# The last block of each attention pair inside the next slot, and its reciprocals by transfer

## The reference, cut to what matters

```python
p = jnp.exp(s - m)
denom = jnp.sum(p, axis=-1, keepdims=True)
if sink is not None:
    denom = denom + jnp.exp(sk - m)
out = jnp.einsum('nbhgqk,nbkhd->nbqhgd', p / denom, vb.astype(jnp.float32))
...
ya = ya.reshape(b, seq, A_W) * jax.nn.silu(za)
```

## Time and profile before

| | |
|---|---|
| runs | 3627.81 us median of 3 (3623.05 to 3629.15) |
| profiled execution | 3626.68 us, its span 3624.9 us |
| PE busy | 3431.3 us (95%) |
| DVE, ACT, POOL busy | 51%, 22%, 33% |
| attention pairs | 1600 to 2140 us (first layer), 2700 to 3165 us (second, roughly) |
| granted TensorE clock, mean | 0.979 |

### The profile page before, as it was taken

How to read it: one execution, slowest core, us unless ns; L and a number is a source line. 1 busy time by engine, 2 the same in 40 slices (tenths; PEclk the granted TensorE clock), 3 DMA queues, 4 the chain that set the end, 5 groups by cost and what they waited for, 6 DMA issues and landing times.

```text
span 3624.9 us, 55702 instructions
## 1 busy us (share of the span) xinstructions
PE 3431.3 (95%) x22740; PEld 2766.9 (76%) x22740; DVE 1858.6 (51%) x2512; ACT 783.5 (22%) x1234; POOL 1186.5 (33%) x557
## 2 busy tenths in 40 slices
PE   5999699999999999989999999999999999999997
PEld 4888489788888888866777678888867677688886
DVE  6531566556666676664544444343545444534434
ACT  3311433211100101133322220000323332300001
POOL 2333054233344344322222224344322222243442
PEclk9999799999999999989999999999999999999998
DMA  3121000121111111131111111111311111111111
GB/s 111 53 69 46 0 4 4 51 87 47 46 46 52 46 46 48 44 112 47 36 35 41 35 70 48 51 46 47 112 53 41 41 35 30 69 47 53 46 46 64
DMA packets 50942, 181.94 MB, mean 50 GB/s; under 512 B 5600, under 2 KB 14304, under 8 KB 49520
## 3 DMA queue, kind: packets, MB, share of 16 engines
q1 hardware_dynamic: 36432, 135.85, 11.8%
q10 hardware_dynamic: 14368, 43.98, 3.6%
HBM read 157.73 MB, written 14.75 MB: 48 GB/s over the span
## 4 chain that ended last, share of the span: by engine, by line
PE 89%; DVE 7%; issue 1%; ACT 1%; DMA 1%; POOL 0%; ACTq 0%; DVEq 0%; SPq 0%; POOLq 0%
PE ps L465 54%; PE ps L901 10%; PE ps L1257 5%; PE ps L1077 3%; PE ps L1104 3%; PE ps L731 3%; PE ps L1122 3%; DVE sc L2486 1%; PE ps L929 1%; PE ps L1143 1%; PE ps L1031 1%; DVE sq_sum L1837 1%; PE ps L484 0%; PE ps L478 0%; DMA pv<-vec 0%
## 5 line engine op out<-in xcount | busy, mean ns | idle before, releaser
L363 POOL TENSOR_TENSOR wH<-wraw,pv 128x1024 fp32r<-128x1024 f32 x239 | 460.5, 1927 | 2183.0 <-PE ps L465 1781.4
L465 PE MATMUL ps<-hH,wH 128*128 128x512 f32 x2800 | 878.1, 395 | 20.8 <-issue 13.6
L465 PE MATMUL ps<-hL,wH 128*128 128x512 f32 x2800 | 870.9, 392 | 0.0
L465 PE MATMUL ps<-hH,wL 128*128 128x512 f32 x2800 | 870.2, 392 | 0.0
L365 POOL TENSOR_TENSOR wL<-wraw,wH 128x1024 fp32r<-128x1024 f32 x239 | 622.8, 2606 | 18.8
L465 PEld LDWEIGHTS ps<-hH,wH 128*128 128x128 f32 x2800 | 523.0, 189 | 136.3 <-issue 24.1
L465 PEld LDWEIGHTS ps<-hL,wH 128*128 128x128 f32 x2800 | 527.5, 189 | 110.5
L465 PEld LDWEIGHTS ps<-hH,wL 128*128 128x128 f32 x2800 | 525.9, 189 | 109.6
L2284 DVE TENSOR_TENSOR xT<-ps,xT 128x512 f32<-128x512 f32 x560 | 372.2, 689 | 11.1 <-PE ps L929 11.0
L2579 DVE TENSOR_TENSOR sg<-ps,mrows 128x1024 f32<-128x1024 f32 x46 | 56.3, 1225 | 371.6 <-PE ps L465 371.6
L1703 ACT ACTIVATE sc<-sc,stat 128x256 f32<-128x256 f32 (+7 forms) x256 | 171.0, 668 | 133.7 <-DVE stat L2493 66.1
(11 more groups left out here) (392 smaller groups left out, 4249.7 us busy)
## 6 DMA issues: line engine op xcount, KB each, us to landing
wraw<-ws SPq DMA_DIRECT2D x242, 512.0 KB, 3.5
park<-xT ACTq DMA_DIRECT2D x2, 4096.0 KB, 13.2
xT<-park ACTq DMA_DIRECT2D x2, 4096.0 KB, 12.9
xT<-xin SPq DMA_DIRECT2D x1, 4096.0 KB, 12.2
xT<-xin ACTq DMA_DIRECT2D x1, 4096.0 KB, 12.2
sc<-kraw ACTq DMA_DIRECT2D x32, 128.0 KB, 2.4
out<-xT SPq DMA_DIRECT2D x8, 512.0 KB, 3.5
sc<-qraw ACTq DMA_DIRECT2D x24, 128.0 KB, 2.4
```

Source lines behind the costliest of these rows:

```text
L363: pool.tensor_tensor(wH[:, j, :], wraw[:, j, :], zero, ALU.add).then_inc(w_hi, 1)
L465: mm = pe.matmul(pair(p)[:, half * HALF:(half + 1) * HALF], wp, hp[:, k, half * HALF:(half + 1) * HALF], start=(m == 0 and n == 0), stop=( ...
```

## The change

- **PE.** `period(7)` and what follows leave the end of the pair. `pair_end` makes three pieces of them: transposes(7, 0) with values(6); transposes(7, 1); values(7) with one transposition of `stat[S_REC]` (16 columns) into 16 rows of bank 4. `col_gemm` of the next query slot (for the last B pair the key slot of `window_keys`) calls them behind its pairs 3, 6 and 11, in C 2, 4 and 8 (from 0). The last C pair of a layer keeps period 7, `rows` and `values(7)` where they were. The transposes of block 7 for head 1 go to PSUM pair 1 instead of 0. The waits for `at_y` stand later: in front of the value transposes (A, B) or of the rotation (C).
- **DVE.** `output` multiplies the PSUM output by the gate alone. A new step `output_scale` multiplies `ypair` by `recT` (the reciprocal rows) once they have come; it and the low part stand behind the query step of the next pair (A), the query rotation (B), the key rotation of `window_keys`, or after blocks 1 and 3 of the next pair (C).
- **ACT.** `spread_reciprocals` copies the 16 rows (`rec_rows`), sends them to a stretch of `out` in DRAM, waits, and issues two transfers that bring each row set to 64 partitions of `recT`. `output_hi` (the high part) moves behind the swap of the queries, before the copy of the keys (B), before the copy of the values (`window_keys`), or after block 3's exponentials (C, at n = 2).
- `qraw2` moves to the place of `vst2`, since `ypair` is alive longer; in B, ACT's copy of the values therefore waits for the query rotation. The C pairs are written out instead of looped. Some semaphores share a name (`gate`, `pool_own`, `rw_tanh`) and nothing else there changes.

```diff
...
-        qraw2 = at("qraw2", XA + 4 * TILE, [P, T])
+        qraw2 = at("qraw2", XA, [P, T])
...
+        rec_rows = at("rec_rows", EX3 + 4 * TILE + 2432, [16, P])
+        recT = at("recT", YL, [P, KT, T])
...
-                col_gemm(0, u)
-                pe.wait_ge(sem("at_y"), pi + 1)
+                col_gemm(0, u, between=pair_end("B", L, 2, 2))
                 col_gemm(1, u)
                 pe.wait_ge(sem("a_raw"), L * 14 + 11)
+                pe.wait_ge(sem("at_y"), pi + 1)
                 pe.wait_ge(sem("a_v"), L * 6 + 6)
...
-                        out, b = pair(0 if n == 7 and j else 2), 0
+                        out, b = pair(1 if n == 7 and j else 2), 0
...
+            def pair_end(br, L, i, first):
+
+                _, transposes, values, _ = steps(br, L, i, first)
+
+                def last_block():
+                    transposes(7, 0)
+                    values(6)
+
+                def values_and_rows():
+                    values(7)
+                    pe.wait_ge(sem("at_rec"), L * 8 + i + (first + 1))
+                    pe.transpose(bank(4)[0:16, 0:P], stat[:, S_REC, :], ident).then_inc(sem("at_rows"), 1)
+
+                at = (2, 4, 8) if br == "C" else (3, 6, 11)
+                return {at[0]: last_block, at[1]: lambda: transposes(7, 1), at[2]: values_and_rows}
+
+            def head_pair(br, L, i, first, ended={}):
+                pi = L * 8 + i + first
+                last = pi * 16
+                scores, transposes, values, period = steps(br, L, i, first)
...
-                pe.wait_ge(sem("at_max"), last + 1)
+                pe.wait_ge(sem("at_max"), last + (2 if br == "C" else 1))
                 if br == "C":
                     u = L * (LAYER_SLOTS // 2) + i + ((SLOT_LAYER + SLOT_WINDOW) // 2 + 1)
-                    col_gemm(0, u)
+                    col_gemm(0, u, between=ended)
 
                     def rotate_q():
                         pe.wait_ge(sem("a_raw"), L * 14 + i + 12)
+                        pe.wait_ge(sem("at_y"), pi + 1)
+                        pe.wait_ge(sem("rec_copied"), spreads(L, i + first))
...
+                        if not leading:
+                            pe.wait_ge(sem("at_y"), pi + 1)
+                            pe.wait_ge(sem("rec_copied"), spreads(L, i + first))
...
-                        col_gemm(*slots[0], p=0)
-
-                        pe.wait_ge(sem("at_y"), pi + 1)
+                        col_gemm(*slots[0], p=0, between=ended)
                         col_gemm(*slots[1], p=1)
...
-                for n in range(within, 8):
+                ends_here = br == "C" and i == 2
+                for n in range(within, 8 if ends_here else 7):
                     period(n)
-                rows()
-                values(7)
+                if ends_here:
+                    rows()
+                    values(7)
...
-                    if br == "A":
+                    if br != "B":
                         for i in range(count):
-                            head_pair(br, L, i, first)
+                            head_pair(br, L, i, first, pair_end(br, L, i - 1, first) if i else {})
                         continue
                     with pe.Fori(0, count) as i:
-                        head_pair(br, L, i, first)
+                        head_pair(br, L, i, first, pair_end(br, L, i - 1, first))
...
+            def output_hi(L, i):
+
+                pi = L * 8 + i
+                act.wait_ge(sem("at_scaled"), pi + 1)
+                act.sem_inc(sem("gate"), 1)
+                act.activation(yH[:, bass.ds(i, 1), :], ypair[:, :].unsqueeze(1), ACT.Copy).then_inc(sem("a_yH"), 1)
+
+            def spread_reciprocals(L, i):
+
+                n = spreads(L, i)
+                act.wait_ge(sem("at_rows"), L * 8 + i + 1)
+                act.activation(rec_rows[:, :], bank(4)[0:16, 0:P], ACT.Copy).then_inc(sem("rec_copied"), 1)
+                act.wait_ge(sem("rec_copied"), n + 1)
+                act.dma_start(out[0:1, 4:6, :].rearrange("o k (r q) -> (o k r) q", q=P), rec_rows[:, :]
+                              ).then_inc(sem("rec_kept"), 16)
+                act.wait_ge(sem("rec_kept"), n * 16 + 16)
+                for j in range(2):
+                    act.dma_start(recT[64 * j:64 * j + 64, bass.ds(i, 1), :],
+                                  out[0:1, 4 + j:5 + j, :].to_broadcast([64, 1, T])).then_inc(sem("rec_spread"), 16)
...
-                act.wait_ge(sem("a_yL"), L * 8 + 6)
+                act.wait_ge(sem("at_y"), L * 8 + 6)
                 act.activation(lnM[:, :], arows[:, :], ACT.Copy)
                 act.wait_ge(gemm_done[0], u + 1)
                 raw_copy(kraw2, 0)
                 swap_halves(kraw2, 1, L * 14 + 11)
+                output_hi(L, 4)
                 act.wait_ge(gemm_done[1], u + 1)
...
                         swap_halves(qraw2, 0, raw + 1)
+                        output_hi(L, i + (first - 1))
...
+                        if n == 2 and i:
+                            output_hi(L, i + (first - 1))
...
-                act.wait_ge(sem("at_y"), pi + 2)
-                act.sem_inc(sem("act_gate"), 1)
-                act.activation(yH[:, bass.ds(i + first, 1), :], ypair[:, :].unsqueeze(1), ACT.Copy).then_inc(sem("a_yH"), 1)
+                if br == "C" and i == 2:
+                    output_hi(L, i + first)
+                else:
+                    spread_reciprocals(L, i + first)
...
+            def output_scale(L, i):
+
+                dve.wait_ge(sem("rec_spread"), spreads(L, i) * 32 + 32)
+                dve.wait_ge(sem("at_y"), L * 8 + i + 2)
+                dve.tensor_tensor(ypair[:, :].unsqueeze(1), ypair[:, :].unsqueeze(1), recT[:, bass.ds(i, 1), :], ALU.mult
+                                  ).then_inc(sem("at_scaled"), 1)
+
+            def output_low(L, i):
+
+                dve.wait_ge(sem("a_yH"), L * 8 + i + 1)
+                dve.tensor_tensor(yL[:, bass.ds(i, 1), :], ypair[:, :].unsqueeze(1), yH[:, bass.ds(i, 1), :],
+                                  ALU.subtract).then_inc(sem("a_yL"), 1)
+
             def window_keys(L):
                 rope(L, L * 10 + 6, L * 14 + 11, swaps(L, 7), SC[1][:, 1, :], SC[1][:, 1, :], kraw2, kP)
+                output_scale(L, 4)
+                output_low(L, 4)
...
+                        if q == 0:
+                            output_scale(L, i + (first - 1))
+                            output_low(L, i + (first - 1))
...
-                    dve.wait_ge(sem("at_rows"), pi + 1)
                     dve.wait_ge(sem("a_z"), pi * 2 + 2)
-                    st.on(dve.tensor_tensor(sz[:, :], pair(1), sz[:, :], ALU.mult))
-                    st.wait(dve)
+                    if ends_here:
+                        dve.wait_ge(sem("at_rows"), pi + 1)
+                        st.on(dve.tensor_tensor(sz[:, :], pair(1), sz[:, :], ALU.mult))
+                        st.wait(dve)
                     dve.wait_ge(sem("at_pv"), pi * 8 + 8)
-                    dve.scalar_tensor_tensor(out=ypair[:, :], in0=pair(3), scalar=0.5, in1=sz[:, :], op0=ALU.mult, op1=ALU.mult
-                                             ).then_inc(sem("at_y"), 1)
+                    ins = dve.scalar_tensor_tensor(out=ypair[:, :], in0=pair(3), scalar=0.5, in1=sz[:, :],
+                                                   op0=ALU.mult, op1=ALU.mult)
+                    ins.then_inc(sem("at_y"), 1)
...
+                    if n == 1 and br == "C" and i:
+                        output_scale(L, i + (first - 1))
+                    if n == 3 and br == "C" and i:
+                        output_low(L, i + (first - 1))
...
```

More of the change, by code:

```diff
@@ L302, in bias_copies, with spreads @@
             return 4 + (L * 2 + i) * 6
+        def spreads(L, i):
+            return L * (KT - 1) + i
         def head_slots(L, br, i):
@@ L386, in _ @@
             zero_slot(SLOT_OUT // 2 - 1)
-            own = Count(sem("pool_own"))
+            own = Count(sem("pool_own"), 1)
             def step(ins):
@@ L649, in gate @@
             def gate():
-                pe.sem_inc(sem("pe_gate"), 1)
+                pe.sem_inc(sem("gate"), 1)
             def rows(q):
@@ L1134, in period @@
                         scores(n + 1)
+                return scores, transposes, values, period
+            def pair_end(br, L, i, first):
[13 more added lines that the diff above has]
+                scores, transposes, values, period = steps(br, L, i, first)
                 def rows():
@@ L2433, in head_pair @@
                 buffers = 4 if br == "C" else 2
-                st = Count(sem("dve_own"), L * 11 + own.n + (i * 2 + 5 if br == "C" else i + first))
+                st = Count(sem("dve_own"), L * 4 + own.n + i)
                 if br == "A":
@@ L2508, in copy_transposed @@
                         dve.wait_ge(sem("at_pv"), pi * 8 + n - 1)
-                    src = bank(5) if n < 4 else pair(2 if n < 7 else 0)
+                    src = bank(5) if n < 4 else pair(2 if n < 7 else 1)
```

49 lines of the change are left out of this document (30 added, 19 removed).

## The result

The changed kernel takes **3578.5 us** (median of 4 runs, 3575.6 to 3578.8), the kernel before in the same session 3625.4 (4 runs): a ratio of 0.987, 95% interval 0.986 to 0.989. Forecast were 3592 us and a range from 3580 to 3606.

A forecast was written before the change was run, and what follows sets the result against it. The prediction took PE (TensorE), 89% of the chain, as the bound. Moved ends gain 38.7 us, less 1.1 and 1.5 is 36.1; from 3626.7 that gives 3590.6, plus 1.1 for the median: 3592 us, range 3580 to 3606.

The forecast's parts named there:

- rival 1: Moved blocks: PE's waits for exponentials and copies move with them into the next slot; 16 us gained, 3612; chance 0.10.
- rival 4: Moved ends: entering and leaving costs 0.11 us more at each of nine switches; about 3617 to 3622; chance 0.04.
- rival 3: Reciprocals' trip through memory is long and delays ACT, DVE, then PE; 3654 us at a 20 us trip; chance 0.04.
- prices of the blocks: PE's moved blocks, priced start to start from the old kernel; A or B end gains 2.72 us, C end 2.88.
- window_keys: ACT's high part of the last B pair delays its values copy, so PE waits: 0.55 us each layer, 1.1 lost.
- The low part in C: C pairs 1 and 2: DVE's low part delays block 5's maxima; 0.37 us, four times, 1.5 lost.
- rival 5: Whole kernel: window_keys and C losses absorbed (2.6 us), two to four slow stretches vanish (up to 6); 3583; chance 0.07.
- 0.1 more a switch: Moved ends on PE: possible extra cost per switch, up to 6 us, part of the forecast's own spread of some 8.
- PE feels it only if ... past 27.8: A or B slot: trip hidden up to 13.8 us unless scale, high part and low part delay ACT's k copy.
- just free: ACT in an A or B slot: held about 5 us by the trip, free when the slot's copy comes at 16.9.
- Of which 25 are the matmuls of L1143: Old pair ends on PE: 25 of 38.7 us gained come from removing 32 small matmuls that spread the reciprocals.
- Rival 2: Thinner, interrupted slots bring one slower-clock stretch per moved end, 1.65 us each; 23 of 36 us lost, 3615; chance 0.05.

The follow-up runs named there:

- second profile of the changed kernel: The changed kernel run again without any edit, with a profile: 3578.1 us, 0.987 of the kernel before.
- The runs with long waits of PE: The changed kernel with four more waited 8 KB writes, ahead of the reads of the reciprocals (3633.9 us) or behind their issue (3640.8 us).

## Where the prediction was right, and which of its steps failed

**Right: the mechanism on PE.** PE sets the time, its blocks find their inputs inside the next slot, the holes do not move with them (rival 1), the returns cost about what was read (rival 4), and the trip stays hidden (rival 3 did not happen).

**Failed: the sizes.** The time fell out of the range on the fast side because terms of the sum were mis-sized, above all the prices of the blocks and the two losses that did not come. The 14 us by which 3592 is too high come from these steps:

1. *Prices of the blocks (A and B ends: 2.72 counted, 3.0 and 3.2 measured).* I priced every block by its place in the kernel before. In front of a gemm the transposes are cheaper: 0.74 and 0.79, where the step "eight transposes 1.02, so seven 0.89" had 0.89 and 1.02. The row transposition takes 0.03 instead of 0.13, the last products 1.90 instead of 1.84. Together 6.11 against 6.58. The returns come to 0.53 in all instead of 0.44, about as read. Ten ends: 31, where the sum had 27.2.
2. *window_keys (1.1 counted, 0 measured).* The step added 1.23 of scale behind the end of the rotation. DVE's operations in a row start every 1.14 us, and that layer's wait for the swap was longer in the profile of before (3.41) than after (2.67). The high part was done 0.3 us before PE had the slot ready.
3. *The low part in C (1.5 counted, 0 measured).* The 0.37 was taken as if all of it reached PE. 0.09 did, and the next wait gave 0.08 back. C ends: 2.80 measured for the end itself (16.84 to 14.04 from the last transposes of block 6 to the query copy; 2.88 counted), 12.0 for four whole pairs where the sum had 10.0. The 2.80 hold a wait that the prediction had at nothing: in front of each of the four slots PE waits 0.24 for the maxima of block 7, for which the edit raised the wait to `last + 2`.
4. *The last C pair of each layer* had no term; it got 0.4 to 0.5 us shorter, twice (34.64 to 34.15 us from its query copy to the merge in the first layer).
5. *The base.* Median and profiled execution of the kernel before lay on the high side of its later runs: 3625.4 over 4 runs, 3623.9 over 19.

2.4 for the base, 3.8 for the blocks, 1.1 and 2.0 for the losses that did not come, and 0.8 make 10.1 of 13.5 us. Some 3 us are left, of which the clock can be 2; the others stay open.

**The range** had room for rival 5 (3583), which was that the losses of steps 2 and 3 are absorbed (they were) and that slow stretches vanish, which the profiles don't show (22.2 against 25.6 and 17.0). What it lacked was an error of the block prices in the gain's direction: "0.1 more a switch" was the only side I had put in.

**The budget was wrong though its outcome was right, and that was luck.** The step "PE feels it only if ... past 27.8", 13.8 us for the trip, took DVE's wait for the rows as what decides. The trip took some 6.5 us where 9 were counted, and no wait of DVE for it is in the trace. Its two transfers (DMA issues: count, KB each, median us to landing):
```profile
recT<-out ACTq DMA_DIRECT2D x28, 256.0 KB, 3.9
...
out<-rec_rows ACTq DMA_DIRECT2D x14, 8.0 KB, 1.4
```
But with about 12 us of trip the gain was already gone. What decides is ACT, held behind its own write: it was free at about 1817.8 and copied the q slot at 1820.3 (second profile of the changed kernel), a room of 2.5 us, and 0.3 to 0.7 us behind the high part at the extra projection. It was held 3.0 us where the prediction had 5 and "just free". The prediction saw that point and did not carry it on. Rival 3 priced 20 us of trip at 3654; 12 us gave 3634. The Trainium skill, DMA: Bandwidth & Descriptors, Anatomy of one DMA, puts about 2 us of fixed cost on a transfer, in its part on transfers that GpSimd issues; the prediction took the figure without that condition. ScalarE issues the 8 KB write here, and it took a median of 1.4 us, so the trace is below the figure.

**"Of which 25 are the matmuls of L1143"** was right for the ends already moved and only so (27.1 measured). Alone in place they bring 5 to 6.

**Rival 2** (the slower level spreads with the switches) falls: 22.2 us not granted in both profiles after, 17.0 and 25.6 before. The runs with long waits of PE had 39 and 49, so the stretches seem to go with waits more than with switches; no run varied the one without the other.

## What to carry to other kernels

Before you take work off the engine that sets the time, look at what waits behind it: matmuls that stand between a transposition and its use may cover the copy, and then their removal pays only once the block stands where other work covers it. A block's price depends on its neighbour in the queue, so price a move with rows that have the new neighbour. And budget a trip through memory by the queue of the engine that waits for its write, not only by who reads the result: here a delay of 1.4 us was nearly free and one of 5.5 us cost the whole gain.

## What the runs showed of the hardware

- The same eight transposes take 0.97 to 1.02 us in front of products and 0.79 in front of a gemm; one of 16 columns costs 0.03 from start to start.
- A write of 8 KB from SBUF to memory lands in 1.4 us (1.3 to 2.2), and five that are each waited for take 6.95 us; behind the issue of two reads of 256 KB four take 8.4 us.
- A DVE operation on two SBUF tensors takes 1.22 us alone and 3.30 beside POOL's split of weights.
- Two executions of the kernel before differ by 7.9 us in their spans and by 8.6 in what the clock did not grant: stretches at 1.2 GHz, 1.4 to 1.7 us each, most of which begin behind PE's waits of 2.4 us (one, at 2084, behind one of 1.25), in one execution at other such waits than in the next. In the changed kernel four of them came back at the same places. That the whole scatter over 12 us is of this kind is not shown.
